# A hybrid attention and state-space block: state products from unscaled C with 128-column weights, growth factors applied by VectorE, and a reordered group and gate stage

## The chip, the cores and the metric

The kernel runs on one core of one Trainium2 chip. The metric is the device time of one execution in microseconds; lower is better. Everything is float32 outside; large matrix products run on operands split into a rounded part and a rest (three products instead of one), small ones run in plain float32.

## The reference

One layer, 512 tokens, width 1024. What matters here is branch B, a chunked state-space scan over 4 groups of 8 heads (64 wide, state 128), and the attention beside it:

```python
cb = jnp.einsum('bclgn,bcsgn->bgcls', cm, bm)
y_diag = jnp.einsum('bgjcls,bcsgjp->bclgjp', cb[:, :, None] * lmat, xdt)
states = jnp.einsum('bcsgn,bcsgjp->bcgjpn', bm, xdt * decay_states[..., None])
# scan over chunks: carry * chunk_decay + states, prev = the carry before each chunk
y_off = jnp.einsum('bclgn,cbgjpn->bclgjp', cm, prev)
y_off = y_off * jnp.transpose(jnp.exp(a_cs), (0, 3, 4, 1, 2))[..., None]
y = y_diag + y_off + x * d_skip...            # then * silu(z), group RMSNorm
merged = sigmoid(gate_a) * (attention @ w_attn_out) + sigmoid(gate_b) * (y @ w_ssd_out)
```

`exp(a_cs)` is the growth factor: one number per head and token. It may be multiplied into C before the product with the state, or into the product. Around it: an input projection, an output projection and a gated feed-forward, each with RMSNorm.

## The kernel before

The kernel is one program per engine, ordered by hand, with named semaphores (`pe.wait_ge(s["y_done"], n)` holds the engine's whole queue). SyncE issues nearly all DMAs. Weights arrive in blocks of up to 128x2048 in two slots `raw`; ScalarE (ACT) makes the rounded part `whi` (`hi`, L482), VectorE (DVE) the rest `wlo` (`lo`, L863), TensorE (PE) multiplies (`tokens` L1299 to L1301, `features` L1292 to L1294).

The program runs over groups `G` = 0 to 3. A group first makes q, k, v (`tokens`), then B, C and x with a causal convolution, then walks over four token tiles `t` of 128. In tile `t`, PE issues, in this order: C times B (L1552), scores (L1565), the tile `t+1` of z (`z_tile`, 24 matmuls), the transposes of the attention probabilities (`turn_p`, L1410), the products of state and `c_dec` (`products`, L1393), those of `xdt` and the masked decay matrix (`diagonal`, L1393 too), B times `xdtd` into PSUM bank 7 for the next state (L1589), and probabilities times v (`weigh_values`, L1422). In tile 3 the last three parts are interleaved with the first q, k, v tiles of the next group; in the last group with the first gate block.

`c_dec` is C times the growth factor of each of 8 heads, 128x1024; GpSimd (POOL) makes it (L444) from `grow_bc`, which a DMA broadcasts. POOL also makes `xdtd` (L439). PE accumulates state products and diagonal products in one PSUM bank (2 or 3, by turns); DVE adds the skip term and writes `yT` (L1113, semaphore `y_done`). DVE then scales `state` (L1120) and adds bank 7 (L1121, `st_ok`). Other DVE steps of a tile: mask of C times B (L1090), row maximum (L1071 to L1074), masked gains (L1062), `xdt` (L1086), division of the probabilities (L1078 to L1080), z gate (L1054), and in tiles 0, 2 and 3 a `lo` (L863). ACT makes the decay matrix (L569 Relu, L575 Exp), the exponentials (L661), copies `pT` and `oT` (L692, L696).

After the groups comes the gate stage: for `i` = 0 to 3 PE multiplies two tiles of gate a (bank 0, 1) and two of `w_attn_out` (bank 2, 3). Its first round also holds what is left of group 3: the sum of squares (`norm_sums`), the mean, the root on POOL, a round trip of the root through DRAM (`spread_roots`) and the multiplication of `yT` by it (`normalize`, L977). In DVE's queue `normalize` stands ahead of the `lo` calls of round 1.

## Time and profile before

| | us |
|---|---|
| median of 3 runs | 1061.54 (1061.15 to 1063.48) |
| the profiled execution, its own time | 1061.45 |
| its span | 1059.7 |
| PE busy | 1033.1 (97%) |
| DVE busy | 640.1 (60%) |
| ACT busy | 472.4 (45%) |
| POOL busy | 86.9 (8%) |

Shares are over the whole span. DVE is busy 71 of 90 us in a group and a third of the time in the gate stage, so the share alone doesn't say where an engine is the limit. A float32 matmul leaves two records; matmul records overlap, so the cost of a piece of PE work is read here from its start to the start of the next piece.

### The profile page before, as it was taken

The numbers are of one execution on the slowest core, as the hardware profiler recorded it, in microseconds if no ns is written. First come the engines' busy times: TensorE is split into PE (matmuls) and PEld (weight loads), VectorE is DVE, ScalarE is ACT, GpSimd is POOL, SyncE is SP. The second block draws the span as 40 slices with busy tenths as digits, with TensorE's granted clock in tenths as the row PEclk, the third lists the DMA queues.
The fourth block names the chain that finished last, engine by engine and source line by source line (L and its number), as shares of the span: only waits on it lengthen the run. The fifth ranks groups of instructions, "written<-read, shape, count | busy, mean of one in ns | idle before, by whom it ended". The sixth has DMA issues, their size and how long they took to land.

```text
span 1059.7 us, 14004 instructions
## 1 busy us (share of the span) xinstructions
PE 1033.1 (97%) x5423; PEld 863.8 (82%) x5423; DVE 640.1 (60%) x851; ACT 472.4 (45%) x835; POOL 86.9 (8%) x132
## 2 busy tenths in 40 slices
PE   8999999999999999989999999999999999999997
PEld 7887888798779877768888888798888888888886
DVE  4878787878787878642523223676766666651214
ACT  5657647655764576512312132554344343422112
POOL 6002101200120021000000003110000000000001
PEclk9999999999999999989999999999999999999999
DMA  6333351343334323232232344421243333332211
GB/s 193 120 126 109 111 148 50 118 133 109 97 103 143 106 100 120 50 111 87 87 112 79 119 158 152 127 71 50 79 114 83 97 101 82 116 119 80 98 62 79
DMA packets 117978, 111.26 MB, mean 105 GB/s; under 512 B 13279, under 2 KB 108075, under 8 KB 117931
## 3 DMA queue, kind: packets, MB, share of 16 engines
q1 hardware_dynamic: 117931, 110.61, 33.8%
q8 instruction: 32, 0.52, 0.2%
q14 instruction: 15, 0.12, 0.0%
HBM read 108.36 MB, written 2.24 MB: 104 GB/s over the span
## 4 chain that ended last, share of the span: by engine, by line
PE 88%; DVE 5%; ACT 3%; DMA 2%; issue 1%; POOL 1%; SPq 0%; DVEq 0%; POOLq 0%; ACTq 0%
PE ps L1292 20%; PE ps L1294 20%; PE ps L1293 20%; PE ps L1299 7%; PE ps L1301 6%; PE ps L1300 6%; PE ps L1393 2%; PE ps L1565 1%; DVE wlo L863 1%; DVE sm L1078 1%; PE ps L1589 1%; DVE state L1120 1%; PE ps L1422 1%; PE ps L1410 1%; ACT x_tok L557 1%
## 5 line engine op out<-in xcount | busy, mean ns | idle before, releaser
L863 DVE TENSOR_TENSOR wlo<-raw,whi 128x2048 fp32r<-128x2048 f32 (+2 forms) x83 | 185.9, 2242 | 198.3 <-ACT whi L482 198.3
L1292 PE MATMUL ps<-uhi,whi 128*128 128x512 f32 x768 | 301.4, 393 | 0.0
L1294 PE MATMUL ps<-uhi,wlo 128*128 128x512 f32 x768 | 299.2, 390 | 0.0
L1293 PE MATMUL ps<-ulo,whi 128*128 128x512 f32 x768 | 298.9, 389 | 0.0
L482 ACT ACTIVATE whi<-raw 128x2048 fp32r<-128x2048 f32 (+2 forms) x83 | 155.8, 1878 | 187.6 <-PE ps L1301 99.0
L1294 PEld LDWEIGHTS ps<-uhi,wlo 128*128 128x128 f32 x768 | 144.2, 188 | 30.4
L1293 PEld LDWEIGHTS ps<-ulo,whi 128*128 128x128 f32 x768 | 144.3, 188 | 29.1
L1292 PEld LDWEIGHTS ps<-uhi,whi 128*128 128x128 f32 x768 | 144.3, 188 | 29.2 <-issue 0.2
L1240 DVE SCALAR_TENSOR_TENSOR yT<-ps,fpar,yT 128x511 f32<-128x511 f32 x88 | 65.8, 749 | 37.5 <-ACT yT L820 35.9
L1292 PE MATMUL ps<-rhi,whi 128*128 128x512 f32 x192 | 75.8, 395 | 6.2 <-DVE wlo L863 6.2
L820 ACT ACTIVATE yT<-ps,fpar 128x512 f32<-128x512 f32 x44 | 34.2, 780 | 98.9 <-DVE fpar L1235 68.0
L1293 PE MATMUL ps<-rlo,whi 128*128 128x512 f32 x192 | 75.6, 394 | 0.0
L1294 PE MATMUL ps<-rhi,wlo 128*128 128x512 f32 x192 | 75.4, 393 | 0.0
L1299 PE MATMUL ps<-whi,rhi 128*128 128x512 f32 x176 | 68.5, 389 | 0.0
L1300 PE MATMUL ps<-whi,rlo 128*128 128x512 f32 x176 | 68.5, 389 | 0.0
L1301 PE MATMUL ps<-wlo,rhi 128*128 128x512 f32 x176 | 68.5, 389 | 0.0
L991 DVE SCALAR_TENSOR_TENSOR conv<-ps,par,conv 128x511 f32<-128x511 f32 (+2 forms) x72 | 53.9, 748 | 18.2 <-ACT conv L545 16.5
L1299 PE MATMUL ps<-whi,uhi 128*128 128x384 f32 (+2 forms) x176 | 64.2, 365 | 0.6 <-DVE wlo L863 0.6
L1301 PE MATMUL ps<-wlo,uhi 128*128 128x384 f32 (+2 forms) x176 | 62.7, 357 | 0.0
L1300 PE MATMUL ps<-whi,ulo 128*128 128x384 f32 (+2 forms) x176 | 62.6, 356 | 0.0
L545 ACT ACTIVATE conv<-ps,par 128x512 f32<-128x512 f32 x24 | 18.7, 778 | 68.7 <-PE ps L1294 68.7
L1292 PEld LDWEIGHTS ps<-rhi,whi 128*128 128x128 f32 x192 | 36.6, 190 | 14.2 <-DVE wlo L863 6.6
(226 smaller groups left out, 1370.5 us busy)
## 6 DMA issues: line engine op xcount, KB each, us to landing
raw<-in_w_in_dram SPq DMA_DIRECT2D x24, 1024.0 KB
raw<-in_w_up_dram SPq DMA_DIRECT2D x44, 512.0 KB
raw<-in_w_down_dram SPq DMA_DIRECT2D x11, 1024.0 KB
raw<-in_w_in_dram SPq DMA_DIRECT2D x16, 512.0 KB
sums_bc<-sum_rows_scratch SPq DMA_DIRECT2D x16, 512.0 KB, 4.2
raw<-in_w_ssd_out_dram SPq DMA_DIRECT2D x8, 1024.0 KB
grow_bc<-sum_rows_scratch SPq DMA_DIRECT2D x12, 512.0 KB, 5.7
raw<-in_w_attn_out_dram SPq DMA_DIRECT2D x4, 1024.0 KB
```

What stands on the lines that cost most here:

```text
L482: act.activation(whi[sl][:, 0:width] if into is None else into, raw[sl][:, 0:width], ACT.Copy).then_inc(s["hi_done"], 1)
L820: act.activation(work[:, v, :], bank(2 * q + v), ACT.Identity, scale=fpar[:, q, FTAPS - 1, v:v + 1], bias=fpar[:, q, FTAPS, v:v + 1]).then ...
L863: dve.tensor_tensor(wlo[sl][:, 0:width] if into is None else into, raw[sl][:, 0:width], h.bitcast(F32), ALU.subtract).then_inc(s["lo_done" ...
L991: ins = dve.scalar_tensor_tensor(out=conv[:, f, sh:], in0=ps[:, 4 + f % 4, 0:S - sh], scalar=cw[:, k, at:at + 1], in1=conv[:, f, sh:], op0 ...
L1240: ins = dve.scalar_tensor_tensor(out=work[:, v, sh:], in0=ps[:, 2 * q + v, 0:S - sh], scalar=fpar[:, q, k, v:v + 1], in1=work[:, v, sh:], ...
L1292: pe.matmul(bank(b)[:, span], hi_[:, k, c], ah[:, span], start=first and k == 0, stop=False)
L1293: pe.matmul(bank(b)[:, span], hi_[:, k, c], al[:, span], start=False, stop=False)
L1294: ins = pe.matmul(bank(b)[:, span], lo_[:, k, c], ah[:, span], start=False, stop=last and k == KD - 1)
L1299: pe.matmul(o, ah, wh, start=first, stop=False)
L1300: pe.matmul(o, al, wh, start=False, stop=False)
L1301: return pe.matmul(o, ah, wl, start=False, stop=last)
L1393: ins = pe.matmul(ps[r, 2 + t % 2, (h // 2) * P:(h // 2 + 1) * P], weights[:, h * HD:(h + 1) * HD], moving[:, h, :], start=first if t == 0 ...
```

## The change

Seven edits, all of them order or form of the same arithmetic:

1. C times B for all four tiles of a group in one go (4 matmuls into bank 6) ahead of `z_tile(0)`, masked by one DVE instruction into `qkv_sb`.
2. State products: 4 matmuls with 128 columns of `state` as weights and C itself moving (`from_state`), into bank 2. DVE multiplies by the growth factors (`grow`) and adds the result to `yT` in a further instruction; PSUM no longer accumulates the two parts. POOL's `c_dec` is gone. `grow_bc` is half as large, double-buffered and filled by two DMAs.
3. B times `xdtd` moves ahead of `turn_p`.
4. `weigh_values` uses 4 matmuls with 128 moving columns instead of 8 with 64, into bank 6; scores no longer wait for the copy `oT`.
5. DVE: the maximum stands ahead of the masked gains; scaling of the state stands ahead of `yT` and waits for `off_mm` (PE done with the old state).
6. State products of tile 3 move behind the next group's first tile.
7. Gate stage: `hi_gate(0)` and the splits of `oT` earlier on ACT, `lo` of round 1 ahead of `normalize` on DVE, the loop over `i` written out, the splits of `yT` spread over it.

```diff
-                    pool.tensor_tensor(c_dec[:, :, :], grow_bc[:, :, :],
-                                       conv[:, 1, (t + 1) * P:(t + 2) * P].unsqueeze(1).to_broadcast([P, SH, P]),
-                                       ALU.mult).then_inc(s["grown"], 1)
...
+                    def grow(t):
+                        n = G * (NT - 1) + t
+                        dve.wait_ge(s[f"grow_in{(n - 1) % 2}"], 32 * ((n + 1) // 2))
+                        dve.tensor_tensor(quarters(from_st), quarters(bank(2)), grow_bc[:, (n - 1) % 2, :, :], ALU.mult).then_inc(s["grown"], 1)
...
-                    masked_cb()
+                    maximum()
                     if t == 0:
+                        dve.wait_ge(s["cbm_ok"], G + 1)
+                    masked_gains()
+                    times_dt()
+                    divide()
...
+                    if 0 < t < NT - 1:
+                        dve.wait_ge(s["off_mm"], G * (NT - 1) + t)
+                        dve.tensor_tensor(h8(state[:, :]), h8(state[:, :]), heads(dec[:, 2, t, group_heads(G)], SH, HD),
+                                          ALU.mult).then_inc(s["scaled"], 1)
+                        grow(t)
+                        dve.wait_ge(s["scaled"], G * (NT - 2) + t)
+                        dve.wait_ge(s["st_mm"], G * (NT - 1) + (t + 1))
+                        dve.tensor_tensor(state[:, :], state[:, :], bank(7), ALU.add).then_inc(s["st_ok"], 1)
                     if t == NT - 1:
-                        lo_next(7, 4 * QKV if G < NG - 1 else BLK)
+                        dve.wait_ge(s["off_mm"], G * (NT - 1) + t)
+                        grow(t)
                     dve.wait_ge(s["y_mm"], T + 1)
...
+                        dve.tensor_tensor(y, quarters(bank(3)), conv[:, 2:6, c], ALU.add).then_inc(s["y_part"], 1)
+                        dve.wait_ge(s["y_part"], G * (NT - 1) + t)
+                        dve.wait_ge(s["grown"], G * (NT - 1) + t)
+                        dve.tensor_tensor(y, y, quarters(from_st), ALU.add).then_inc(s["y_done"], 1)
...
+            for at in range(5):
+                split_o(at)
+            gate_y(NG - 1)
+            for at in range(5, KD):
+                split_o(at)
+            lo(0, N_C1 + 3)
+            sum_squares(NG - 1)
+            gate_a(0)
+            for k in range(KD):
+                split_y(k)
+            gate_a(1)
             normalize(NG - 1)
...
+                for half in (1, 0):
+                    cols = slice(64 * half, 64 * half + 64)
+                    v = qkv_sb[:, t, QW + KW:QW + 2 * KW] if half else va[:, t, :]
+                    for a in range(2):
+                        o = ps[64 * a:64 * a + 64, 6, 0:2 * P].rearrange("p (f c) -> p f c", f=2)[:, :, cols]
+                        ins = pe.matmul(o, v, pT[:, 2 * a:2 * a + 2, cols], start=True, stop=True)
                 ins.then_inc(s["o_mm"], 1)
+
+            def from_state(G, t):
+                pe.wait_ge(s["st_ok"], G * (NT - 1) + t)
+                pe.wait_ge(s["grown"], G * (NT - 1) + t - 1)
+                if t == 1:
+                    pe.wait_ge(s["tok_sb"], G * 5 + 1)
+                for f in range(4):
+                    c = slice(f * P, (f + 1) * P)
+                    ins = pe.matmul(ps[:, 2, c], state[:, c], conv[:, 1, t * P:(t + 1) * P], start=True, stop=True)
+                ins.then_inc(s["off_mm"], 1)
...
                     elif t == 2:
-                        pe.wait_ge(s["y_done"], G * NT - 1)
+                        pe.wait_ge(s["grown"], G * (NT - 1))
...
                     if t < NT - 1:
                         z_tile(t + 1)
-                        turn_p(G, t)
-                    if t:
-                        pe.wait_ge(s["st_ok"], G * (NT - 1) + t)
-                        pe.wait_ge(s["grown"], G * (NT - 1) + t)
-                        if T > 1:
-                            pe.wait_ge(s["y_done"], T - 1)
-                        if t == 1:
-                            pe.wait_ge(s["tok_sb"], G * 5 + 3)
-                        products(G, t, state, c_dec, True, False)
-                    if t < NT - 1:
-                        diagonal(G, t)
                         pe.wait_ge(s["xdtd_ok"], G * (NT - 1) + t + 1)
                         if t:
                             pe.wait_ge(s["st_ok"], G * (NT - 1) + t)
                         else:
                             pe.wait_ge(s["tok_sb"], G * 5 + 5)
                         pe.matmul(bank(7), b_tok[:, c], xdtd[:, :], start=True, stop=True).then_inc(s["st_mm"], 1)
+                        turn_p(G, t)
+                        if t:
+                            from_state(G, t)
+                        diagonal(G, t)
                         weigh_values(G, t)
```

PE's queue in tile 1 of a group, behind `z_tile(2)`, before the change (the first row is `turn_p`, the last is the scores of tile 2; the eight L1422 rows are `weigh_values`):

```order
L1410 MATMUL ps<-ident,probs 128x128 x4
L1393 MATMUL ps<-c_dec,state 64x128 x8
L1393 MATMUL ps<-decay_m,xdt 64x128 x8
L1589 MATMUL ps<-xdtd,b_tok 128x512
L1422 MATMUL ps<-pT,qkv_sb 64x64
L1422 MATMUL ps<-pT,va 64x64
...
L1552 MATMUL ps<-conv 128x128
L1565 MATMUL ps<-kB,qB 128x128 x4
```

and of the change, at the same place:

```order
L1622 MATMUL ps<-xdtd,b_tok 128x512
L1443 MATMUL ps<-ident,probs 128x128 x4
L1469 MATMUL ps<-conv,state 128x128 x4
L1435 MATMUL ps<-decay_m,xdt 64x128 x8
L1459 MATMUL ps<-pT,qkv_sb 64x2x64 x2
L1459 MATMUL ps<-pT,va 64x2x64 x2
L1609 MATMUL ps<-kB,qB 128x128 x4
```

B times `xdtd` now stands first, C times B is gone from here, and the products with the state are four with full-width weights.

DVE's queue in the same tile, from the z gate on, before:

```order
L1054 SCALAR_TENSOR_TENSOR zg<-tanh_c,ps 128x512
L1113 TENSOR_TENSOR yT<-ps,conv 128x4x128
L1120 TENSOR_TENSOR state<-state,dec 128x512
L1121 TENSOR_TENSOR state<-state,ps 128x512
L1090 TENSOR_TENSOR cb_m<-ps,tri 128x128
L1071 TENSOR_REDUCE sm<-ps 128x4
```

and of the change:

```order
L1076 SCALAR_TENSOR_TENSOR zg<-tanh_c,ps 128x512
L1131 TENSOR_TENSOR state<-state,dec 128x512
L1106 TENSOR_TENSOR from_st<-ps,grow_bc 128x512
L1136 TENSOR_TENSOR state<-state,ps 128x512
L1146 TENSOR_TENSOR yT<-ps,conv 128x4x128
L1149 TENSOR_TENSOR yT<-yT,from_st 128x4x128
L1092 TENSOR_REDUCE sm<-ps 128x4
```

Two instructions of 128x512 are new, one of 128x128 is gone, and the state is renewed ahead of `yT`.

DVE's queue behind the last group, before:

```order
L1130 TENSOR_TENSOR rlo<-oT,rhi 128x512 x8
L960 TENSOR_TENSOR yT<-yT,zg 128x512 x4
L1134 SCALAR_TENSOR_TENSOR rlo<-yT,par,rhi 128x512 x4
L965 TENSOR_TENSOR conv<-conv 128x512 x3
L863 TENSOR_TENSOR wlo<-raw,whi 128x2048
L1153 SCALAR_TENSOR_TENSOR oT<-gt,ps 128x512 x2
L977 TENSOR_TENSOR yT<-yT,conv 128x512 x4
L1134 SCALAR_TENSOR_TENSOR rlo<-yT,par,rhi 128x512 x4
```

and of the change (L995 is `normalize`, L881 is `lo`, L1180 the gate):

```order
L1162 TENSOR_TENSOR rlo<-oT,rhi 128x512 x5
L978 TENSOR_TENSOR yT<-yT,zg 128x512 x4
L1162 TENSOR_TENSOR rlo<-oT,rhi 128x512 x3
L881 TENSOR_TENSOR wlo<-raw,whi 128x2048
L983 TENSOR_TENSOR conv<-conv 128x512 x3
L1180 SCALAR_TENSOR_TENSOR oT<-gt,ps 128x512 x2
L1166 SCALAR_TENSOR_TENSOR rlo<-yT,par,rhi 128x512 x8
L881 TENSOR_TENSOR wlo<-raw,whi 128x2048 x2
L1180 SCALAR_TENSOR_TENSOR oT<-gt,ps 128x512 x2
L995 TENSOR_TENSOR yT<-yT,conv 128x512 x4
```

Two `lo` now stand ahead of `normalize`.

## Rows read from the trace of the kernel before

**Rows 1.** The page: busy time of each engine.

```profile
PE 1033.1 (97%) x5423; PEld 863.8 (82%) x5423; DVE 640.1 (60%) x851; ACT 472.4 (45%) x835; POOL 86.9 (8%) x132
```

**Rows 2.** PE's waits: for whom, us in total, times, longest.

```profile
PE ps L1393 <- DVE state L1121: 3.1, 4, 1.2
PE ps L1410 <- DVE probs L1080: 2.6, 4, 0.7
...
PE ps L1422 <- ACT pT L692: 0.7, 1, 0.7
```

**Rows 3.** Timeline of PE, group 1, tile 0's end to tile 1: start, us.

```profile
188.29 0.49 PE L1552 MATMUL ps<-conv 128*128 128x128 f32 x2
188.88 1.13 PE L1565 MATMUL ps<-kB,qB 128*128 128x128 f32 x8
189.76 0.48 PE L1292 MATMUL ps<-uhi,whi 128*128 128x512 f32 x1
...
195.32 0.60 PE L1410 MATMUL ps<-ident,probs 128*128 128x128 f32 x4
195.85 1.09 PE L1393 MATMUL ps<-c_dec,state 128*64 128x128 f32 x16
196.77 1.04 PE L1393 MATMUL ps<-decay_m,xdt 128*64 128x128 f32 x16
197.74 1.13 PE L1589 MATMUL ps<-xdtd,b_tok 128*128 128x512 f32 x2
198.80 0.34 PE L1422 MATMUL ps<-pT,qkv_sb 128*64 128x64 f32 x4
...
199.46 0.49 PE L1552 MATMUL ps<-conv 128*128 128x128 f32 x2
```

**Rows 4.** Timeline of all engines, group 1, tile 2's end to tile 3.

```profile
207.93 1.75 DVE L863 TENSOR_TENSOR wlo<-raw,whi 128x1536 fp32r<-128x1536 f32 x1
...
209.14 1.13 PE L1589 MATMUL ps<-xdtd,b_tok 128*128 128x512 f32 x2
209.34 1.28 ACT L569 ACTIVATE decay_m<-sums_bc,sum_s 128x128 f32<-128x128 f32 x4 [1.39 <-PE ps L1393]
...
210.97 0.38 ACT L696 ACTIVATE oT<-ps 128x256 f32<-128x256 f32 x1 [0.34 <-PE ps L1422]
...
212.41 1.14 ACT L575 ACTIVATE decay_m<-decay_m 128x512 f32<-128x512 f32 x2
...
213.28 0.68 DVE L1071 TENSOR_REDUCE sm<-ps 128x4 f32<-128x512 f32 x1
...
214.25 0.44 PE L1299 MATMUL ps<-whi,uhi 128*128 128x384 f32 x1
...
214.48 1.29 DVE L1062 TENSOR_TENSOR decay_m<-decay_m,cb_m 128x512 f32<-128x512 f32 x2
...
216.53 1.09 PE L1393 MATMUL ps<-decay_m,xdt 128*64 128x128 f32 x16
```

**Rows 5.** Timeline of POOL and DVE in group 1, tiles 0 and 1.

```profile
181.53 2.41 POOL L444 TENSOR_TENSOR c_dec<-grow_bc,conv 128x1024 f32<-128x1024 f32 x1
181.55 2.41 DVE L1078 TENSOR_TENSOR sm<-sm 128x4 f32<-128x4 f32 x1 [0.60 <-ACT sm L663]
...
198.00 2.35 POOL L444 TENSOR_TENSOR c_dec<-grow_bc,conv 128x1024 f32<-128x1024 f32 x1 [3.63 <-PE ps L1393]
...
198.91 1.99 DVE L1120 TENSOR_TENSOR state<-state,dec 128x512 f32<-128x512 f32 x1 [0.35 <-PE ps L1589]
...
200.94 0.69 DVE L1121 TENSOR_TENSOR state<-state,ps 128x512 f32<-128x512 f32 x1
```

**Rows 6.** Timeline of DVE and PE in the gate stage.

```profile
446.44 4.03 DVE L977 TENSOR_TENSOR yT<-yT,conv 128x512 f32<-128x512 f32 x4 [7.60 <-DMA conv<-roots_scratch]
450.37 2.75 DVE L1134 SCALAR_TENSOR_TENSOR rlo<-yT,par,rhi 128x512 fp32r<-128x512 f32 x4
453.02 4.50 DVE L863 TENSOR_TENSOR wlo<-raw,whi 128x2048 fp32r<-128x2048 f32 x2
...
455.38 0.80 PE L1292 MATMUL ps<-rhi,whi 128*128 128x512 f32 x1 [6.18 <-DVE wlo L863]
```

**Rows 7.** Ten us of the gate stage: busy us of PE, PEld, DVE, ACT, POOL, then PEclk, the granted clock.

```profile
455.00:465.00 10.00, 9.62 (x32) 7.74 (x33) 3.21 (x3) 0.00 (x0) 0.00 (x0) 0.74 0.64 210
```

More of the change, by code:

```diff
@@ L123, in hybrid_block @@
         ones = sb("ones", [P, P], where=gctx)
-        cb_m = sb("cb_m", [P, P], where=gctx)
         sum_s = sb("sum_s", [P, NT, NH], where=gctx)
@@ L705, in _, with split_y, gates_a @@
             act.wait_ge(s["o_sb"], NG * NT)
[L706 to L707 removed]
+            for k in O_ORDER[5:]:
+                split_o(k)
             SN = 0
[L709 to L714 removed]
+            def split_y(k):
+                act.activation(rhi[:, Y_TILE[k], :], yT[:, k, :], ACT.Copy, scale=par[:, 1, SN + k:SN + k + 1]).then_inc(s["split_hi"], 1)
+            def gates_a(i):
                 n = i * 2 + N_C1
[L716 to L717 removed]
                 for m in range(2):
@@ L1115, in group @@
[L1115 to L1121 removed]
+                    y = yT[:, G * 4:G * 4 + 4, c]
@@ L1284, in tiles, with features @@
                 return w.rearrange("p (k n) -> p k n", k=k)
-            def features(b, sl, m, acts, first=True, last=True, span=slice(0, S), split=None):
+            def features(b, sl, m, acts, first=True, last=True, span=slice(0, S), split=None, ks=tuple(range(KD))):
                 hi_, lo_ = (tiles(w, KD) for w in split or (whi[sl][:, :], wlo[sl][:, :]))
-                for k in range(KD):
+                for k in ks:
                     ah, al = acts(k)
                     c = slice(m * P, (m + 1) * P)
-                    pe.matmul(bank(b)[:, span], hi_[:, k, c], ah[:, span], start=first and k == 0, stop=False)
+                    pe.matmul(bank(b)[:, span], hi_[:, k, c], ah[:, span], start=first and k == ks[0], stop=False)
                     pe.matmul(bank(b)[:, span], hi_[:, k, c], al[:, span], start=False, stop=False)
-                    ins = pe.matmul(bank(b)[:, span], lo_[:, k, c], ah[:, span], start=False, stop=last and k == KD - 1)
+                    ins = pe.matmul(bank(b)[:, span], lo_[:, k, c], ah[:, span], start=False, stop=last and k == ks[-1])
                 return ins
@@ L1387, in _ @@
             stream(3)
-            def products(G, t, weights, moving, first, last):
-                for h in range(SH):
-                    r = slice((h % 2) * HD, (h % 2 + 1) * HD)
-                    ins = pe.matmul(ps[r, 2 + t % 2, (h // 2) * P:(h // 2 + 1) * P], weights[:, h * HD:(h + 1) * HD],
-                                    moving[:, h, :], start=first if t == 0 else first and h < 2, stop=last if t == 0 else last and h >= SH - 2)
-                return ins
             def diagonal(G, t):
@@ L1400, in diagonal @@
                 pe.wait_ge(s["xdt_ok"], T + 1)
+                pe.wait_ge(s["y_done"], T)
                 if t == 0:
-                    pe.wait_ge(s["y_done"], max(T - 1, 0))
-                    pe.wait_ge(s["tok_sb"], G * 5 + 1)
-                products(G, t, xdt, decay_m, t == 0, True).then_inc(s["y_mm"], 1)
+                    pe.wait_ge(s["tok_sb"], G * 5 + 3)
+                for h in range(SH):
+                    r = slice((h % 2) * HD, (h % 2 + 1) * HD)
+                    ins = pe.matmul(ps[r, 3, (h // 2) * P:(h // 2 + 1) * P], xdt[:, h * HD:(h + 1) * HD], decay_m[:, h, :],
+                                    start=True, stop=True)
+                ins.then_inc(s["y_mm"], 1)
             def turn_p(G, t):
@@ L1540, in group @@
                 tok(1)
+                pe.wait_ge(s["silu_ok"], G * 6 + 2)
+                pe.wait_ge(s["conv_ok"], G * 6 + 3)
+                for t in range(NT):
+                    c = slice(t * P, (t + 1) * P)
+                    ins = pe.matmul(ps[:, 6, c], conv[:, 0, c], conv[:, 1, c], start=True, stop=True)
+                ins.then_inc(s["cb_mm"], 1)
+                z_tile(0)
                 for t in range(NT):
```

187 lines of the change are left out of this document (89 added, 98 removed).

## Prediction

> **What bounds the kernel now.** I read the page first: PE is busy 1033.1 of 1059.7 us [rows 1]. So a change can gain in three ways only: less PE work, fewer of PE's waits, or a clock that isn't lowered. Next the waits of PE [rows 2], then the timeline of one tile [rows 3], of the seam between two groups [rows 4], of POOL beside DVE [rows 5], and of the gate stage, where one single wait stands out [rows 6, 7]. The other engines matter where PE waits for them and nowhere else.
>
> In the timeline a piece costs PE its start to the next start. Tile 1 reads: C times B 0.59 us, scores 0.88 (four matmuls of 128x128, so 0.22 each), z tile 5.56, `turn_p` 0.53, state products 0.92, diagonal 0.97, B times `xdtd` 1.06, `weigh_values` 0.66 [rows 3]. PE hardly idles inside.
>
> **PE work, part by part.**
>
> C times B. Three times per group it costs 0.59, a fourth time 0.22 if it costs what a score does: 1.99. Four in a row, by the price of a score: 0.88. Less by 1.1, four groups: **-4.4**. Part of the 0.59 is that the scores wait for the copy `oT`; that wait leaves the scores too, so the whole 0.59 goes. Bounds: if four together cost 0.3 each, -3.1; nothing speaks for more than -4.4.
>
> State products. Eight half-width matmuls now cost 0.92, four full-width ones 4 x 0.22 = 0.88 by the scores, which have the same form. Twelve times: **-0.5**. The two halves evidently ran at the same time already, for 0.92 is not twice 0.88. The Trainium skill, TensorEngine Tiling (Array Packing), "Key Properties", says that different tiles can execute weight loads and matmuls in parallel, and the row agrees. Its section "The Problem" says that the full array is underused where the left operand's free dimension is at most 64; read alone, that promises half the time here, which is the last rival below.
>
> `weigh_values`. Four matmuls of the diagonal's form (64-column weights, 128 moving) cost half of 0.97, which is 0.49; nothing gained would be 0.66. I take 0.55, nearer to the form that it will have, with something for starting a small piece. Sixteen times 0.11: **-1.8** (0 to -2.7).
>
> B times `xdtd`. Its 512 columns are as many as the four scores have, 0.88, yet it costs 1.06 between two half-width pieces. Moved between full-width pieces it may cost 0.88. I take a bit over half of the difference, 0.1, twelve times: **-1.2** (0 to -2.2).
>
> **Waits that go.** PE waits 3.1 us for the state in tile 3, four times, 2.6 us for the probabilities in tile 0, four times, and 0.7 us once for `pT` [rows 2]: **-6.4** in all. The tile 0 wait has an odd cause: a DVE instruction on 128x4 elements takes 2.41 us while POOL's `c_dec` runs, and ends with it. In the same way `state` times `dec` takes 1.99 us beside `c_dec`, while the addition right behind it, as large, takes 0.69 [rows 5]. `c_dec` is gone, so I price both at what they cost alone, and `grow` and the second addition to `yT` at 0.69 too. DVE thus pays two new instructions, 1.4 us a tile, and gets back 1.3 us of scaling and a mask; POOL keeps only `xdtd`. The Trainium skill, SBUF — State Buffer, "SBUF: two separate sides", calls the port pair of the two engines "an exclusive lock, not a bandwidth split", which these rows bear out. The state wait goes as PE now asks for the state only after a whole q, k, v tile (2.28 us, 214.25 to 216.53 [rows 4]) where it waited up to 1.2. The single `pT` wait is covered by a tile of gate a (as long as one of z, 5.56) placed ahead of `weigh_values`.
>
> **Waits that come.** Let D be the end of tile 2's diagonal (209.14 [rows 4]). ACT starts the next decay matrix at D+0.2: four Relus 1.2, the copy `oT` 0.3, four Relus 1.2, so Exp starts at D+2.9 (3.27 before, when the copy waited 0.34). Its first half is done at D+3.5. DVE: PE is done with the old state at about D-1; scale, grow, add, `yT`, add, five times 0.69, end at D+2.5, and the maximum takes 1.2 (213.28 to 214.48), D+3.7, if `lo` of tile 2 (1.75) found its room before; it stands between the division and the z gate, where DVE waits for z now, and just fits. Masked gains 1.2, `xdt` 0.69: done at about D+5.5. PE: 0.55 + 0.88 + 2.28 + 0.88, ready at D+4.6. So PE waits 0.9 us ahead of the diagonal of tile 3, in groups 0 to 2 (in group 3 a whole tile of gate a stands between). Then 0.97 for the diagonal, 2.28 for the next tile, 0.53 for `turn_p`: PE is at D+9.3 at the q, k, v tile that now needs `grow` of tile 3. DVE has the division (one 128x512 instruction and two tiny ones, some 1.2), `lo` 1.75 and grow 0.69 behind D+5.5; I add 0.6 as `lo` waits for ACT's `hi`, D+9.8. Wait 0.5. Together 1.4, three groups: **+4.2** (0 to 9). The inner tiles stay free of waits: PE's next z tile ends at D + 0.55 + 0.88 + 5.56 = D+7.0, and B times `xdtd` needs POOL, which starts at D+5.5 and has half the size of `c_dec`, so half of 2.35: D+6.7. This margin of 0.3 is the thin place of the change.
>
> **The gate stage.** PE waits 6.18 us for one `lo`. DVE had been held by `normalize`, which waited 7.60 us for the root's trip through DRAM, took 4.03, and had 2.75 of splits behind it, and only then came the `lo` [rows 6]. In the new order that `lo` stands ahead of `normalize`. What stands ahead of it there: splits, gate, `lo`, 8 splits of `yT` (0.69 each, 5.5). By my walk it is done some 3 us before PE asks. What is late next? `normalize` itself, but its result is asked for only by the products with `w_ssd_out`, over 30 us later; and the SyncE queue, where the next gate block's load stands behind the root's trip as it did before. **-6.2**. After the wait PE's clock is granted at 0.74 on average over ten us [rows 7], that is 5.2 us at the lower of its two levels (1.2 against 2.4 GHz). Matmul for matmul that is half of 5.2 minus what fell in the wait: **-2.4**. The Trainium skill, TensorE: Matmul & The Clock Gate, "What's actually happening", ties the level to how busy PE has been; the trace agrees, as PE was idle just before. Without a wait I expect no low stretch there.
>
> **Sum.** -4.4 - 0.5 - 1.8 - 1.2 - 6.4 + 4.2 - 6.2 - 2.4 = -18.7. The profiled execution took 1061.45 (span 1059.7 and 1.75 around it), 0.09 less than the median of the runs. 1061.45 - 18.7 = 1042.75, so **1043**. The bounds of the unknown costs: all at their worse ends give +1.3, +1.8, +1.2 and +4.8, 1052; at their better ends -0.9, -1.0, -4.2, 1037; they won't all fall one way, so its own range is 1038 to 1048.
>
> **Rivals.** A change of 0.2%, 2.1 us, is about what a measurement of this kernel can tell from none.
>
> (a) The gate stage still waits: DVE's eight splits and the gate ahead of `lo` come later than I walk, by over 3 us, and the same wait and low clock come back. For it: DVE waited 7.60 us there, so its queue is set by waits I have read only in part. Time 1043 + 8.6 = 1051.6.
>
> (b) DVE becomes the limit inside a group: scaling the state costs 1.99 for its own sake, not because of POOL. Then the chain behind D is 1.3 later, against margins near 0: 1.1 us of waiting in tile 1 and 1.3 in tile 2's seam, 8 to 9 us in all groups: 1051.5. Against it: the 128x4 instruction, which can't be slow by itself.
>
> (c) Slower than before: the new VectorE form as a whole doesn't fit. If scale, grow and the additions, four a tile, each take twice 0.69 (like what happens beside POOL), the chain is 2.8 later in tiles 1 and 2, 8 times, 22 us: 1065. It decides from 2.6 us a tile on (20.8/8), of which (b) alone is half. For it there is only the contention with `xdtd`, which stays, at another place.
>
> (d) (a) and (b) together: 1060, within 0.2%.
>
> (e) Full-width weights halve the state products: 0.46 less, twelve times, instead of 0.5 in all: 1038. Against it: the scores' 0.22 each.
>
> **Chances.** Forecast 0.67, (a) 0.11, (b) 0.09, (c) 0.06, (d) 0.03, (e) 0.04. Faster by over 0.2%: all but (c) and (d), 0.91; same 0.03; slower 0.06. A range of 1037 to 1052.5 takes in the forecast's, (a), (b) and (e), and leaves out (c), (d) and some of the tails.
>
> **What would show it.** PE's waits: no `wlo` wait over 2 us in the gate stage and no granted clock under 1.00 there; none for `probs` in tile 0; a new one for `xdt` or `decay_m` ahead of the diagonal of tile 3, near 0.9, and one for `from_st`, near 0.5, three times each. State times `dec` at 0.69; C times B four in 0.9; `weigh_values` near 0.55; B times `xdtd` near 0.95. I am wrong if POOL isn't what slows the state, if a wait before B times `xdtd` shows in each tile, or if the gate stage waits at another block.

## The result and the profile after

The changed kernel takes 1038.84 us (median of 4 runs, 1037.54 to 1039.97) against 1062.32 (median of 4, 1061.15 to 1063.48) for the kernel before, run beside it: ratio 0.9779, 95% interval 0.976 to 0.9798. The forecast was 1043 (1037 to 1052.5); the gain of 23.5 us is some 4 us more than forecast. The profiled execution has its own time of 1039.66 and a span of 1037.9 us.

The page after, the line that answers to [rows 1] and, behind it, the chain that ended last by engine:

```profile
PE 1021.4 (98%) x5199; PEld 863.6 (83%) x5199; DVE 635.4 (61%) x863; ACT 470.5 (45%) x835; POOL 58.0 (6%) x120
...
PE 90%; DVE 4%; ACT 3%; issue 1%; POOL 1%; DMA 1%; DVEq 0%; POOLq 0%; SPq 0%; ACTq 0%
```

PE's busy time fell by 11.7 of the 21.8 us by which the span fell. The rest is idle time of PE, mostly waits. PE's waits after, as [rows 2] (for whom, us in total, times, longest):

```profile
PE ps L1435 <- DVE decay_m L1083: 2.6, 3, 0.9
PE ps L1346 <- ACT yT L799: 2.2, 1, 2.2
```

The long wait for `wlo` in the gate stage (6.2, [rows 6]) and those for the state (3.1), the probabilities (2.6) and `pT` (0.7) are gone. The one that came is that for the gains ahead of tile 3's diagonal, three times 0.9. The wait for `yT` was 1.1 before. Now PE's timeline of group 1: its one C times B (C·B from here on), then tile 0's end to tile 2, which answers to [rows 3]; the price of a piece is its start to the next start:

```profile
168.92 1.06 PE L1593 MATMUL ps<-conv 128*128 128x128 f32 x8
169.74 0.48 PE L1329 MATMUL ps<-uhi,whi 128*128 128x512 f32 x1
...
185.81 1.16 PE L1609 MATMUL ps<-kB,qB 128*128 128x128 f32 x8
...
192.27 1.02 PE L1622 MATMUL ps<-xdtd,b_tok 128*128 128x512 f32 x2
193.12 0.60 PE L1443 MATMUL ps<-ident,probs 128*128 128x128 f32 x4
193.56 1.06 PE L1469 MATMUL ps<-conv,state 128*128 128x128 f32 x8
194.55 1.09 PE L1435 MATMUL ps<-decay_m,xdt 128*64 128x128 f32 x16
195.47 0.39 PE L1459 MATMUL ps<-pT,qkv_sb 128*64 128x128 f32 x4
195.69 0.39 PE L1459 MATMUL ps<-pT,va 128*64 128x128 f32 x4
196.01 1.16 PE L1609 MATMUL ps<-kB,qB 128*128 128x128 f32 x8
```

B times `xdtd` now costs 0.85 (1.06), `turn_p` 0.44 (0.53), the state products 0.99 (0.92), the diagonal 0.92 (0.97), `weigh_values` 0.54 (0.66); the C·B in between is gone, and one of 0.82 (four matmuls) stands ahead of z once per group. A tile repeats after 10.20 us (185.81 to 196.01) and took 11.17 (188.88 in [rows 3] to the next scores at 200.05).

VectorE in the same group, beside [rows 5]: the 128x4 operation of tile 0 and the scaling of the state in tile 1 are short.

```profile
179.89 0.16 DVE L1099 TENSOR_TENSOR sm<-sm 128x4 f32<-128x4 f32 x1
...
194.65 0.69 DVE L1131 TENSOR_TENSOR state<-state,dec 128x512 f32<-128x512 f32 x1 [0.87 <-PE ps L1469]
```

The gate stage, the same operations as [rows 6], and ten us of it as [rows 7] (busy us of each engine, then the granted clock):

```profile
429.25 2.29 DVE L881 TENSOR_TENSOR wlo<-raw,whi 128x2048 fp32r<-128x2048 f32 x1
438.07 2.29 DVE L881 TENSOR_TENSOR wlo<-raw,whi 128x2048 fp32r<-128x2048 f32 x1 [6.53 <-ACT whi L482]
...
446.67 4.05 DVE L995 TENSOR_TENSOR yT<-yT,conv 128x512 f32<-128x512 f32 x4
```

```profile
445.00:455.00 10.00, 10.00 (x46) 8.29 (x45) 6.86 (x6) 2.52 (x2) 0.00 (x0) 1.00 0.08 23
```

The low parts of the weights come ahead of the normalisation, PE has no wait in the list from here up to that for `yT` at 660 us, and its clock is granted in full (1.00, that is 2.4 GHz). The `lo` that PE had waited for ends at 431.5; where the old order is put back (below), PE is there at 435.4.

Where the 21.8 us of span went, by PE's marks in the two traces (first C·B of group 0, and the norm sums of the last group in the gate stage): up to the first C·B 1.5 us more (72.08, then 73.56), a part that the change doesn't touch and in which the first C·B of the runs below comes between 71.7 and 74.1; from there to the end of the norm sums 15.6 less (365.9 to 350.3); from there to the end 7.6 less, of which 8.7 is the gate stage and -1.1 the longer wait for `yT`. The forecast had 10.1 for the groups and 8.6 for the gate stage. So it is the groups that gave more than forecast.

### The profile page after: what moved, and what is told of

The parts are those of the page before. It is cut to its first block, busy times and chain, and to the rows that moved or that the text cites. A ratio compares the mean times of both kernels' runs of the same rounds, so it can differ in the third digit from the quotient of the medians.

```text
span 1037.9 us, 13508 instructions
## 1 busy us (share of the span) xinstructions
PE 1021.4 (98%) x5199; PEld 863.6 (83%) x5199; DVE 635.4 (61%) x863; ACT 470.5 (45%) x835; POOL 58.0 (6%) x120
## 4 chain that ended last, share of the span: by engine, by line
PE 90%; DVE 4%; ACT 3%; issue 1%; POOL 1%; DMA 1%; DVEq 0%; POOLq 0%; SPq 0%; ACTq 0%
PE ps L1329 21%; PE ps L1331 21%; PE ps L1330 21%; PE ps L1336 7%; PE ps L1338 6%; PE ps L1337 6%; PE ps L1435 1%; PE ps L1609 1%; DVE wlo L881 1%; PE ps L1573 1%; PE ps L1622 1%; ACT decay_m L572 1%; PE ps L1368 1%; DMA raw<-in_w_up_dram 1%; PE ps L1443 1%
## 5 line engine op out<-in xcount | busy, mean ns | idle before, releaser
L881 DVE TENSOR_TENSOR wlo<-raw,whi 128x2048 fp32r<-128x2048 f32 (+2 forms) x83 | 185.9, 2241 | 197.1 <-ACT whi L482 197.0
L572 ACT ACTIVATE decay_m<-sums_bc,sum_s 128x128 f32<-128x128 f32 x128 | 40.3, 389 | 13.4 <-PE ps L1435 13.4
```

What stands on the lines that cost most here:

```text
L572: ins = act.activation(decay_m[:, h, :], sums_bc[:, h, :], ACT.Relu, scale=-1.0, bias=sum_s[:, t, at:at + 1])
L881: dve.tensor_tensor(wlo[sl][:, 0:width] if into is None else into, raw[sl][:, 0:width], h.bitcast(F32), ALU.subtract).then_inc(s["lo_done" ...
```

## The experiments

Medians of the changed kernel were 1038.84 and, run once more, 1037.72. Its groups repeat after 95.34 us of the trace (C·B of group 1 at 168.92, of group 2 at 264.26), those of before after 98.64. The start varies by over 2 us and the stretch behind the groups by another 2, so for small effects I give this period too: in most kernels here it is the same for all three groups that have a next one, to 0.04.

**The gate order, undone.** The changed kernel with one line put back.

```diff
-            gate_a(1)
             normalize(NG - 1)
+            gate_a(1)
             gate_a(2)
```

> The changed kernel with one line of VectorE's order put back: the last group's normalisation (about 4 us, ending a wait for a transfer from memory) again ahead of gate 1's two rests instead of behind them. Theory of the prediction: the low parts of gate 1's weights are late again, TensorE waits some 4 to 6 us ahead of gate 1 and its clock falls for a while, so the time is 1045 to 1048 us (6 to 8.6 above the changed kernel's 1038.8). Rival: the wait went because the whole tail of the last group was brought forward and the scalar engine's order was changed, not because of this line; then the time stays within 2 us of 1038.8.

Measured 1045.6 (1044.59 to 1046.61), 6.8 slower than the changed kernel; period 95.33, unchanged. By the traces the stretch from the norm sums up to the wait for `yT` grows by 6.0. PE waits again, and the clock of the ten us behind is granted at 0.83:

```profile
PE ps L1329 <- DVE wlo L881: 4.1, 1, 4.1
```

```profile
430.00:440.00 10.00, 5.94 (x27) 4.62 (x26) 6.79 (x6) 3.10 (x3) 0.00 (x0) 1.00 0.49 128
440.00:450.00 10.00, 10.00 (x39) 8.04 (x38) 2.33 (x2) 0.00 (x0) 0.00 (x0) 0.83 0.65 210
```

**The gate order alone, in the kernel before.**

```diff
             gate_a(0, True)
+            gate_a(1)
             normalize(NG - 1)
             for k in range(KD // 2, KD):
                 split_y(k, KD + k + 1)
-            with dve.Fori(1, NG) as i:
-                gate_a(i)
+            gate_a(2)
+            gate_a(3)
```

> The kernel before with one line of the change alone: VectorE does gate 1's two rests and products ahead of the last group's normalisation and second half of the rests of y, instead of behind them. Nothing else of the changed kernel. Theory: the whole loss at gate 1 (a wait of 6.2 us and a clock of 1.2 GHz behind it for some us) is that order's, so it goes alone: 1053 to 1055 us. Rival: it needs the scalar engine's new order of splits as well; then gate 1 still waits, and the time is 1059 us or more.

Measured 1052.9 (1052.69 to 1054.38) against 1061.5, ratio 0.992 (0.9905 to 0.9935): 8.6 us, and no wait for `wlo` over 0.6 is left. One call moved in VectorE's order is over a third of the whole gain. The new order of splits on the scalar engine isn't needed for it.

**GpSimd's scaling of C shortened, in the kernel before.**

```diff
+                    few = slice(0, SH if T == 0 else 1)
-                    pool.tensor_tensor(c_dec[:, :, :], grow_bc[:, :, :],
-                                       conv[:, 1, (t + 1) * P:(t + 2) * P].unsqueeze(1).to_broadcast([P, SH, P]),
+                    pool.tensor_tensor(c_dec[:, few, :], grow_bc[:, few, :],
+                                       conv[:, 1, (t + 1) * P:(t + 2) * P].unsqueeze(1).to_broadcast([P, SH, P])[:, few, :],
```

> The kernel before with GpSimd scaling C for one of the eight heads instead of all (all eight for the very first tile, so the other heads of later tiles are stale: part of the computation is left out, nothing else changes). Theory: beside a short GpSimd operation VectorE scales the state in 0.69 instead of 1.99 us, the state is in time, and the four waits of TensorE for it at tile 3 (3.1 us) go; the waits for the probabilities at tile 0 stay: 1058.5 to 1059.5 us. Rival: the state scaling is long by itself, and nothing moves: 1061.5 to 1062.7 us.

This kernel leaves out the scaling of seven of the eight heads, in every tile but the first. Measured 1054.98 (1054.54 to 1056.33), 6.5 us less than the 1061.5 beside it: over twice what I expected. The state scaling takes 0.69, and not only the four waits for the state are gone but also those for the probabilities but one, that of tile 0 in group 0, where GpSimd still has its full work. The period falls from 98.64 to 96.89. DVE in group 1 of this kernel, first the small operation of [rows 5], then the scaling:

```profile
182.08 0.46 DVE L1079 TENSOR_TENSOR sm<-sm 128x4 f32<-128x4 f32 x1 [0.60 <-ACT sm L664]
...
198.57 0.69 DVE L1121 TENSOR_TENSOR state<-state,dec 128x512 f32<-128x512 f32 x1 [0.35 <-PE ps L1590]
```

0.46 beside a GpSimd operation of 0.46, and 2.41 beside one of 2.41: it ends when that ends. In tile 1, with GpSimd idle, it takes 0.16 in this kernel and in the one before. So both waits in the groups had this one cause, and rival (b), a scaling that is long by itself, is out.

**GpSimd's work given back, in the changed kernel.**

```diff
                                        ALU.mult).then_inc(s["xdtd_ok"], 1)
+                    pool.wait_ge(s["silu_ok"], G * 6 + 2)
+                    pool.wait_ge(s["y_mm"], T + 1 if t else T)
+                    for r in range(2):
+                        pool.wait_ge(s["beside"], 2 * (T - G) + r)
+                        pool.tensor_tensor(spare, ones[:, :].unsqueeze(1).to_broadcast([P, 4, P]),
+                                           tri[:, :].unsqueeze(1).to_broadcast([P, 4, P]), ALU.mult).then_inc(s["beside"], 1)
```

> The changed kernel with GpSimd given back as much work as the removed scaling of C: behind each of its products xdt times decay two products of 128x512 that nobody reads (about 1.2 us each), started by the same event as the old one. Theory of the prediction: VectorE's state scaling runs beside them and takes near 2.0 us again instead of 0.69, the state is late and TensorE waits for it at tiles 2 and 3: 6 to 8 waits of about 0.9 us, the time 1044 to 1047 us. Rival 1: the 1.99 us is the operation's own length with these operands; then nothing changes in it beside GpSimd, it already reads 0.69 here, which would speak against that from the start. Rival 2: GpSimd's operations cost VectorE nothing on the path since the state has slack now; the time stays within 1 us of 1038.8 though the scaling is long.

Measured 1045.38 (1045.02 to 1047.14), 6.5 slower: the size is as forecast, the place is not. The order of VectorE has changed, so the state scaling is over before GpSimd starts, and stays at 0.69. What is hit is the second addition to `yT`. DVE and POOL in group 1, tile 1:

```profile
194.57 0.69 DVE L1139 TENSOR_TENSOR state<-state,dec 128x512 f32<-128x512 f32 x1 [0.87 <-PE ps L1478]
...
196.37 0.68 DVE L1154 TENSOR_TENSOR yT<-ps,conv 128x512 f32<-128x512 f32 x1
197.09 1.81 DVE L1157 TENSOR_TENSOR yT<-yT,from_st 128x512 f32<-128x512 f32 x1
```

```profile
195.70 2.65 POOL L453 TENSOR_TENSOR from_st<-ones,tri 128x512 f32<-128x512 f32 x2 [3.82 <-issue]
```

L1154 and L1157 both lie beside GpSimd's pair. The one that takes an operand from PSUM (`ps`) costs 0.68, the one with both from SBUF 1.81. The Trainium skill, SBUF — State Buffer, "SBUF: two separate sides", says that of VectorE's operations it is those with two SBUF inputs (or in a two-port mode) that compete with GpSimd; these two rows agree. Thereby the gains of tile 3 are masked later, and PE's waits:

```profile
PE ps L1444 <- DVE decay_m L1091: 5.8, 3, 2.0
PE ps L1631 <- POOL xdtd L447: 2.6, 4, 0.6
```

3.2 more at the first, 2.6 new at the second, together 5.8 of the 6.5. The second is ahead of B times `xdtd`, the thin margin that the prediction named. But GpSimd isn't late by its own work, it is idle for 3.7 us before: `xdtd` of tile 2 starts at 202.08 instead of 201.10, as VectorE's longer addition delivers `xdt` 0.98 later. This profile also shows one stretch at a lower granted clock (0.66 over 310 to 315 us), behind the third of three waits of 1.9 to 2.0 for `decay_m`; the period there is 98.57, that of the two groups ahead 97.1.

**C times B once per group, in the kernel before.** The products, the mask and the waits of bank 6 alone; the scores still wait for the copy `oT`.

```diff
-                    pe.matmul(bank(6, P), conv[:, 0, c], conv[:, 1, c], start=True, stop=True).then_inc(s["cb_mm"], 1)
                     if t == 0:
+                        for a in range(NT):
+                            ca = slice(a * P, (a + 1) * P)
+                            ins = pe.matmul(ps[:, 6, ca], conv[:, 0, ca], conv[:, 1, ca], start=True, stop=True)
+                        ins.then_inc(s["cb_mm"], 1)
                         z_tile(0)
...
                     if t:
                         pe.wait_ge(s["o_sb"], T)
```

> The kernel before with C times B computed once for all four tiles of a group, into a whole bank, and masked once, as in the change; the scores still wait for the copy of the tile's attention output, with which they share a bank. Additive reading, that of the prediction's sum: 4.4 us less, about 1057.7 us. Rival: the product of each tile lay over that wait (the copy ends 0.1 us before the scores start at 200.05), so the wait shows in its place, 0.5 us at three tiles of each group, while the one product for the group costs 0.8 instead of 0.15: no gain or up to 3 us slower, 1061.5 to 1065 us.

Measured 1064.57 (1063.77 to 1066.38, 10 runs) against 1061.5, ratio 1.0029 (1.002 to 1.0039): 3 us slower. The rival holds. PE and ACT in group 1 of this kernel:

```profile
202.09 0.34 PE L1421 MATMUL ps<-pT,qkv_sb 128*64 128x64 f32 x4
...
202.86 0.38 ACT L696 ACTIVATE oT<-ps 128x256 f32<-128x256 f32 x1 [0.35 <-PE ps L1421]
...
203.34 1.13 PE L1563 MATMUL ps<-kB,qB 128*128 128x128 f32 x8 [0.52 <-issue]
```

From the start of `weigh_values` to the scores it is 1.25 with the product (0.66 and 0.59, [rows 3]) and 1.25 without it. The profile names no releaser for the 0.52 (`issue`), but the scores' code waits for the copy `oT`, which ends at 203.24, 0.1 us ahead of them. So the 0.59 of a C·B was time in which PE would have waited for the copy; only the new bank of the attention output, in the change, sets it free. The group's product costs 0.81 in place of the first tile's 0.14, hence the loss; the period is 99.27.

**The old wait put back, in the changed kernel.**

```diff
                     if t:
-                        pe.wait_ge(s["pT_sb"], T)
+                        pe.wait_ge(s["o_sb"], T)
```

> The changed kernel with the scores of tiles 1 to 3 waiting again for the copy of the previous tile's attention output, as before the change (they need it no longer, the output has another bank). Theory: the copy stands behind four of the scalar engine's gains and ends 1.3 us after the scores start now, so TensorE waits that long nine to twelve times, less the 0.9 us that tile 3 waits in three groups anyway: 1048 to 1053 us. Rival: the copy would come about as early as before the change (0.1 us ahead of need once no product fills the place: 0.5 us each): 1043 to 1045 us.

Measured 1051.89 (1051.72 to 1055.11), 13 slower. PE waits ahead of the scores 12 times, 16.0 us in all, 1.34 each; the wait ahead of tile 3's diagonal shrinks from 0.88 to 0.26. The period is 98.62 to 98.66, that of the kernel before.

```profile
PE ps L1609 <- issue: 16.0, 12, 1.3
```

```profile
200.06 0.36 ACT L702 ACTIVATE oT<-ps 128x256 f32<-128x256 f32 x1
...
200.52 1.13 PE L1609 MATMUL ps<-kB,qB 128*128 128x128 f32 x8 [1.34 <-issue]
```

The only new condition of the scores is the copy, and they start 0.1 us behind its end. So the copy comes later behind `weigh_values` than it did. In both kernels four Relus on the scalar engine (1.28 us) start at the end of the diagonal and stand ahead of it. Before, B times `xdtd` lay between diagonal and `weigh_values`, so the Relus were done and the copy started 0.77 us behind the first product of `weigh_values` (198.80, 199.57), after a wait of 0.34 for the last. Now `weigh_values` follows the diagonal at once, and the copy starts 1.48 behind (195.47, 196.95). Taking the wait off the scores therefore gives more than C·B's 0.59: with the wait left in, the move of B times `xdtd` brings the copy later in the tile's course, and all that the groups had gained is lost again.

**B times `xdtd` put back behind the diagonal, in the changed kernel.**

```diff
-                        pe.matmul(bank(7), b_tok[:, c], xdtd[:, :], start=True, stop=True).then_inc(s["st_mm"], 1)
                         turn_p(G, t)
                         if t:
                             from_state(G, t)
                         diagonal(G, t)
+                        pe.matmul(bank(7), b_tok[:, c], xdtd[:, :], start=True, stop=True).then_inc(s["st_mm"], 1)
                         weigh_values(G, t)
```

> The changed kernel with the product of B and xdtd (one matmul with 128-column weights and 512 columns moving) put back behind the diagonal products, which have 64-column weights, from its place behind z. Theory: it takes 1.06 us there instead of 0.85, because the weights' width changes on either side of it, 12 times, and state and growth come later by 1.6 us: 1041 to 1043 us, with a wait for the state at tile 3 of about 0.6 us in each group. Rival: its place costs nothing and the 1.06 was a wait in disguise; then the time stays within 1 us of 1038.8.

The product moves with its waits (the diff leaves them out). Measured 1042.65 (1041.14 to 1042.81), 3.8 slower. Group 1, tile 1:

```profile
192.42 0.60 PE L1443 MATMUL ps<-ident,probs 128*128 128x128 f32 x4
192.86 1.06 PE L1469 MATMUL ps<-conv,state 128*128 128x128 f32 x8
193.84 1.09 PE L1435 MATMUL ps<-decay_m,xdt 128*64 128x128 f32 x16
194.87 1.12 PE L1626 MATMUL ps<-xdtd,b_tok 128*128 128x512 f32 x2
195.92 0.44 PE L1459 MATMUL ps<-pT,qkv_sb 128*64 128x128 f32 x4
```

The product costs 1.05 instead of 0.85, the diagonal ahead of it 1.03 instead of 0.92, and `weigh_values` behind 0.59 instead of 0.54: 0.36 a tile, 12 times 4.3. Against it the wait ahead of tile 3's diagonal falls to 0.58 and the one for the growth product goes, so the period is 95.89, and by the traces the four groups are 2.8 longer in all. The rest of the 3.8 is within the scatter outside them. I had priced only the product itself, and had expected a wait for the state at tile 3, which didn't come.

**State products with half-width weights, in the changed kernel.**

```diff
-                for f in range(4):
-                    c = slice(f * P, (f + 1) * P)
-                    ins = pe.matmul(ps[:, 2, c], state[:, c], conv[:, 1, t * P:(t + 1) * P], start=True, stop=True)
+                for h in range(SH):
+                    r = slice((h % 2) * HD, (h % 2 + 1) * HD)
+                    ins = pe.matmul(ps[r, 2, (h // 2) * P:(h // 2 + 1) * P], state[:, h * HD:(h + 1) * HD],
+                                    conv[:, 1, t * P:(t + 1) * P], start=True, stop=True)
```

> The changed kernel with its state products as eight matmuls with 64-column halves of the state as weights (128 columns of C moving in each) instead of four with 128-column weights; C is still unscaled and the growth still multiplied in behind. Theory of the prediction: a set of these costs about the same either way (0.92 us before for eight, 0.99 after for four, 12 sets), so the time is 1037 to 1040 us. Rival, the one that had full width halve the set: each set takes 0.4 to 0.5 us more than now, 12 sets, the time 1043.5 to 1045 us.

Measured 1036.86 (1036.07 to 1038.28), just under what was expected. Rival (e) is out: full width isn't half the price. Group 1, tile 1:

```profile
192.09 0.60 PE L1443 MATMUL ps<-ident,probs 128*128 128x128 f32 x4
192.62 1.09 PE L1469 MATMUL ps<-conv,state 128*64 128x128 f32 x16
193.54 1.04 PE L1435 MATMUL ps<-decay_m,xdt 128*64 128x128 f32 x16
194.42 0.39 PE L1459 MATMUL ps<-pT,qkv_sb 128*64 128x128 f32 x4
```

The state products cost 0.92 (0.99 at full width) and the diagonal 0.88 (0.92), but `turn_p` ahead of them 0.53 (0.44): sum 2.33 against 2.35. The switch from full to half width costs about 0.1 here, in either place, and is read in the piece ahead of it. The period is 95.33, so the groups have no difference, although the median lies 2.0 below that of the changed kernel.

**The changed kernel once more**, for that difference.

> The changed kernel once more, unchanged. The kernel with half-width state products was 2.0 us faster by its median though its groups take the same time in the trace. If that is scatter of the parts outside the groups (start, one wait near 660 us, clock behind it), the changed kernel has profiles with such a start too, its groups again repeat every 95.3 us, and its median lies anywhere from 1036.5 to 1040 us. If half-width products are truly faster, it stays at 1038.3 to 1039.3 us and the range of its runs lies above 1037.5.

Measured 1037.72 (1037.29 to 1040.06), period 95.34; its profiled execution has its first C·B at 71.75 instead of 73.56. About half of the 2.0 is gone. 0.9 between the medians stays, within the scatter of either kernel's runs; the traces show no place for it.

**`weigh_values` with eight matmuls, in the changed kernel.**

```diff
-                for half in (1, 0):
-                    cols = slice(64 * half, 64 * half + 64)
...
-                        ins = pe.matmul(o, v, pT[:, 2 * a:2 * a + 2, cols], start=True, stop=True)
+                for h in range(QH):
+                    r = slice((h % 2) * 64, (h % 2) * 64 + 64)
+                    for half in (1, 0):
+                        o = ps[r, 6, (h // 2) * P + 64 * half:(h // 2) * P + 64 * half + 64]
...
+                        ins = pe.matmul(o, v, pT[:, (h % 2) * 2 + h // 2, 64 * half:64 * half + 64], start=True, stop=True)
```

> The changed kernel with the values weighed by eight matmuls with 64 moving columns, as before, instead of four with 128; everything else as changed. Theory (the prediction's term, 1.8 us): 0.66 instead of 0.53 to 0.59 us in 16 places, 1.5 to 2 us slower than the changed kernel, 1040.3 to 1040.8 us, about as much as a run's own scatter. Rival: the four are short only because z's first product no longer waits for a switch behind them; then the seam stays and the time is within 0.5 us of 1038.8.

Measured 1042.8 (1040.88 to 1043.01), 4 to 5 slower, which is more than either theory said. The groups show only part of it: 0.61 instead of 0.54 in tiles 0 to 2, 0.66 instead of 0.59 in tile 3, 0.03 more in the z tile behind; the period is 95.65, 1.3 us in four groups. Behind the groups this profile has a stretch at a lower granted clock (0.91 between 660 and 680 us) right after the wait of 2.2 us for `yT` (PE's busy time, then the granted clock):

```profile
660.00:680.00 20.00, 17.22 (x108) 0.91 0.20 54
```

In the profiled execution of the changed kernel, with the same wait, that stretch reads 1.00. It is 1.6 us of the span; what decides whether it comes is open. So of the term's 1.8 us this bears out 1.3.

**The diagonal of the last tile one tile later, in the changed kernel; and with VectorE's growth product ahead of `lo`.** The first edit alone, then both:

```diff
                             from_state(G - 1, NT - 1)
-                            diagonal(G - 1, NT - 1)
                         elif h == 0 and t == 1:
+                            diagonal(G - 1, NT - 1)
                             turn_p(G - 1, NT - 1)
```

```diff
                     if t < NT - 1:
                         gate(t + 1)
                     else:
+                        dve.wait_ge(s["off_mm"], G * (NT - 1) + t)
+                        grow(t)
                         lo_next(7, 4 * QKV if G < NG - 1 else BLK)
...
-                    if t == NT - 1:
-                        dve.wait_ge(s["off_mm"], G * (NT - 1) + t)
-                        grow(t)
```

> The changed kernel with the last tile's diagonal products moved from behind the next group's tile 0 to behind its tile 1 (groups 0 to 2), so that TensorE has a tile's work while VectorE masks the gains. Simple reading: the three waits of 0.9 us for the mask go, 2.6 us less, 1036 us. Theory from the order on VectorE: tile 2 needs bank 2 free, and the growth product that frees it stands behind the low parts of a weight block and ends at about 215.0 in group 1, while TensorE would be there at 213.9; so about 1 us of wait appears at tile 2 and the time stays at 1038 to 1039.5 us.

> As the kernel with the diagonal behind tile 1, and VectorE's growth product of the last tile moved ahead of the low parts of the weight block (1.8 us), which TensorE needs only some 4 us later. Theory: both the wait for the mask and the one for bank 2 go, and with them the 0.2 us that tile 2 waits now: 0.9 to 1.2 us less in each of three groups, 1035 to 1036.2 us, below the changed kernel by about 3. Rival: the sum of y comes too late for tile 3 then, which waits for it instead by 0.5 to 1 us in each group: 1037 to 1038.5 us.

The first alone: 1038.03 (1037.69 to 1040.19), nothing, period 95.35. The wait has changed its name:

```profile
PE ps L1336 <- DVE from_st L1106: 3.2, 3, 1.1
```

Both: **1034.32** (1034.03 to 1034.58), ratio to before 0.9741 (0.9728 to 0.9755), the fastest kernel here; the whole range lies 2.7 us or more below the lowest run of the changed kernel, and a little below the expected 1035 to 1036.2. The period is 94.05, 1.29 less in each of three groups. DVE in group 1, tile 3: growth now stands ahead of the 1.75 us of `lo`.

```profile
209.53 0.69 DVE L1101 TENSOR_TENSOR probs<-probs,sm 128x512 f32<-128x512 f32 x1
210.14 0.68 DVE L1106 TENSOR_TENSOR from_st<-ps,grow_bc 128x512 f32<-128x512 f32 x1
210.74 1.75 DVE L881 TENSOR_TENSOR wlo<-raw,whi 128x1536 fp32r<-128x1536 f32 x1
212.41 0.68 DVE L1145 TENSOR_TENSOR yT<-ps,conv 128x512 f32<-128x512 f32 x1
```

Between the first C·B and the wait for `yT` PE's list has no wait any more, and none for the sum of y came at tile 3.

## Why the prediction was right, step by step

**The gate stage** (-6.2 and -2.4): right in place, cause and size. The order alone gives 8.6 in the kernel before; undone in the changed kernel it costs 6.8 (6.0 by the trace), because the wait is then 4.1 and not 6.2: four splits of `yT`, 2.75 us in [rows 6], no longer stand between `normalize` and the `lo`. Rival (a) is out.

**Waits that go** (-6.4): right, and the cause is shown. The prediction let the state wait go for two reasons (cheaper scaling, and a tile ahead of the request); the first alone does it, and takes the waits for the probabilities along. Short GpSimd operations are worth 6.5 us in the kernel before. 5.1 of it are the listed waits (3.1 for the state, 2.0 for the probabilities in groups 1 to 3); the rest, 0.4 in each group, is in the pieces next to a wait or a late operand (in group 1 the z tile ahead of the wait costs 6.39 with it, 0.15 more than 5.58 and the 0.66; the z tile issued in tile 2 costs 5.71 and then 5.55). Such seams were no term of the sum. With the new VectorE order the probabilities would be in time even beside a busy GpSimd, as the kernel with the work given back shows. What edits 5 and 6 give by themselves (the rest of VectorE's order, and the state products of tile 3 a tile later) was not run.

**C times B** (-4.4): the size is right, 1.91 to 0.82 in a group, 4.4 in all. But it isn't a gain of fewer products. The reason that the prediction gave in half a sentence (the wait for `oT` leaves the scores) is the whole of it: without it the edit costs 3 us.

**B times `xdtd` moved** (-1.2): of the terms for PE's products the one most in error. The product gives 0.2 in each of 12 places, 2.4, and its neighbours 0.15 each, together 4.3 by the trace of the kernel that puts it back; net of the waits at tile 3, which the move makes longer, 2.8 by the trace and 3.8 in the measured time. The step "I take a bit over half of the difference" failed, and so did looking at one piece only: what costs is the switch of width on both sides, and in the old place it stood between two half-width pieces.

**State products** (-0.5): wrong in sign, small. 0.99 and not 0.88, +0.6 over twelve, as the switch to half width that stood ahead of them now stands behind; it is given back in `turn_p` (0.53 to 0.44). The kernel with half-width products shows that the form is worth nothing either way.

**`weigh_values`** (-1.8): right in size, 1.8 by the traces, but not all by its new form. Some 0.05 of the 0.12 a tile is the place behind B times `xdtd` (0.59 there, 0.54 behind the diagonal); undoing the form alone costs 1.3.

**Waits that come** (+4.2): 0.9 ahead of tile 3's diagonal came as said, three times 0.88. The 0.5 for the growth product came as 0.3 (`turn_p` of tile 3 to tile 2 of the next group costs 0.64 against 0.36). In the inner tiles nothing came, and the margin of 0.3 ahead of B times `xdtd` held; VectorE's `xdt` 0.98 later, beside a busier GpSimd, was enough to break it.

**The sum.** Forecast for the groups -10.1, measured -15.6. Added up over PE's pieces in both traces, from the first C·B to the end of the last norm sums, each wait counted as a wait:

| | forecast | measured |
|---|---|---|
| C·B | -4.4 | -4.4 |
| state products | -0.5 | +0.6 |
| `weigh_values` | -1.8 | -1.8 |
| B times `xdtd` | -1.2 | -2.4 |
| waits that go | -6.4 | -6.4 |
| waits that come (2.6 and 0.8) | +4.2 | +3.5 |
| `turn_p` -1.4, diagonal -0.8, scores -0.6, tiles of q, k, v, z and gate a -1.8 | 0 | -4.6 |

The last row is most of the miss. None of these products was changed, and the forecast put each at nothing. The first three stand next to a switch of width or a late operand; for the 1.8 of the tiles that is shown only in part.

That the time still fell inside the range is in part luck. The traces give 15.6 and 8.7 less, which would be 1037.2, at the very edge of the range's 1037; 1.5 more at the start and 1.1 more at `yT`, neither of them foreseen, hid about half of the miss in the profiled execution.

## What to carry to other kernels

When PE is 97% busy, ask of every short piece whether it is work or the cover of a wait: take it out alone and see whether the wait appears. Put pieces with weights of the same width next to each other, and price a move by its neighbours as well. And a wait that is moved, not removed, takes the name of whatever stands next in the other engine's queue; look at what long operation stands ahead of the one now asked for, and let the short one pass.

## What the runs showed of the hardware

- A switch between full-width (128 columns of weights) and half-width (64) pieces costs PE 0.1 to 0.2 us, read mostly in the piece ahead. Full to half: `turn_p` takes 0.53 ahead of half-width state products and 0.44 ahead of full-width ones; B times `xdtd` takes 1.05 ahead of half-width `weigh_values` and 0.85 ahead of full-width `turn_p`. Half to full: the diagonal takes 1.03 ahead of B times `xdtd` and 0.92 ahead of `weigh_values`. The changed kernel has two such switches in tile 1, the one before had four.
- Beside a GpSimd operation VectorE's time depends on where the operands lie: 1.81 us with both in SBUF, 0.68 with one in PSUM, the same size. A 128x4 operation took 2.41 beside one of 2.41, 0.46 beside one of 0.46, and 0.16 with GpSimd idle. GpSimd pays too: its pair of products took 2.65 us in tile 1 and 5.04 in tile 0, where VectorE divided the probabilities and made a `lo` at the same time (2.79 for the `lo`, 2.28 in the changed kernel).
- After the wait of 4.1 us the granted clock was 0.83 over ten us. After the wait of 2.2 near 660 us it was 0.91 over twenty in one profile and 1.00 in another. With more work on GpSimd one execution had a wait of 1.9 to 2.0 us at the same place of three groups, and only behind the third was the clock lower (0.66 over five us).
